# Two transformer blocks on one core: all layers in two passes over half of the tokens, with the expert rows of the first half beside the second pass

## What is computed

```python
def reference(x, ...):
    x = first_block(x, mem, ...)      # in-projection, 8 forgetting heads, 8 chunked heads, out-projection,
                                      # cross attention to a memory of 256 rows, feed-forward 1024-4096-1024
    return second_block(x, c_2, ...)  # modulation from c (6 x 1024), in-projection, sliding-window attention,
                                      # gated linear attention, out-projection, experts, last norm

def peer_ffn(h, wq, subkeys, u, v):   # the experts: 16,384 of them, 8 heads, 16 chosen by each head and token
    ...
    ub = jnp.take(u, eb, axis=0)                                   # 128 rows of 4 KB for each token
    hid = gelu(einsum('tkd,td->tk', ub, xb)) * gb
    vb = jnp.take(v, eb, axis=0)                                   # and 128 more
    return einsum('tk,tkd->td', hid, vb)
```

## Time and profile before

| what | value |
|---|---|
| median of 3 runs | 2741.86 us (2736.21 to 2760.91) |
| span of the profiled execution | 2733.2 us, clock of TensorE granted 0.935 |
| its own time beside the span | the span leaves out what lies around the program; the median of the runs is 8.7 us above it |
| PE, DVE, ACT, POOL busy | 2263.1, 1475.1, 645.8, 1188.2 us |
| moved by DMA | 665 MB, of them 537 MB by POOL's gathers |
| first gather issued, last gather issued | 1201.3 us, 2715.2 us from the start |

### The profile page before, as it was taken

How to read it: one execution, slowest core, us unless ns; L and a number is a source line. 1 busy time by engine, 2 the same in 40 slices (tenths; PEclk the granted TensorE clock), 3 DMA queues, 4 the chain that set the end, 5 groups by cost and what they waited for, 6 DMA issues and landing times.

```text
span 2733.2 us, 27506 instructions
## 1 busy us (share of the span) xinstructions
PE 2263.1 (83%) x9564; PEld 1445.1 (53%) x9564; DVE 1475.1 (54%) x3398; ACT 645.8 (24%) x1548; POOL 1188.2 (43%) x1128
## 2 busy tenths in 40 slices
PE   7999999999999999896977776767777777676775
PEld 6876888889979877665532222322223222232222
DVE  2435232375573425779866664557654567644434
ACT  3225332421120435422121111111111211111111
POOL 5200222110000221325566666666676666766664
PEclk9999999999999999898989998999988999988899
DMA  4211131144452222048889999999999999999998
GB/s 140 78 47 63 63 123 70 70 175 173 186 201 91 78 78 78 32 175 311 310 333 354 359 363 363 367 367 355 363 374 354 358 379 364 373 364 367 372 362 308
DMA packets 170936, 665.46 MB, mean 243 GB/s; under 512 B 19632, under 2 KB 20160, under 8 KB 160320
## 3 DMA queue, kind: packets, MB, share of 16 engines
q0 software_dynamic: 147456, 536.94, 52.1%
q1 hardware_dynamic: 23360, 127.00, 12.7%
HBM read 661.76 MB, written 2.10 MB: 243 GB/s over the span
## 4 chain that ended last, share of the span: by engine, by line
PE 42%; POOL 20%; DVE 15%; issue 10%; another core or an unknown queue 9%; ACT 2%; DMA 1%; SPq 0%; POOLq 0%; DVEq 0%; ACTq 0%
POOL area L544 11%; PE bank L1034 9%; PE bank L1035 9%; PE bank L1036 9%; POOL weights L535 8%; DVE weights L1925 6%; PE bank L1489 4%; PE bank L1076 2%; PE bank L1132 2%; PE bank L1187 1%; PE bank L1206 1%; PE bank L1093 1%; PE bank L1115 1%; PE bank L1099 1%
## 5 line engine op out<-in xcount | busy, mean ns | idle before, releaser
L1431 PE MATMUL bank<-area,gain_row 128*128 128x512 f32 x1888 | 967.3, 656 | 368.5 <-issue 204.2
L1431 PEld LDWEIGHTS bank<-area,gain_row 128*128 128x128 f32 x1888 | 366.6, 207 | 962.3 <-issue 824.1
L1925 DVE CUSTOM_DVE_ANT_0 weights<-weights,bank 128x1024 f32<-128x1024 f32 x504 | 596.9, 1218 | 346.7 <-DMA weights<-in_peer_u,scratch 241.0
L544 POOL DMA_INDIRECT area<-in_peer_v,scratch x512 | 491.5, 960 | 269.4 <-issue 142.3
L535 POOL DMA_INDIRECT weights<-in_peer_u,scratch x504 | 482.5, 957 | 261.4 <-issue 146.7
L918 ACT ACTIVATE gain_row<-ident,scratch 128x128 f32<-128x128 f32 x472 | 178.5, 398 | 1082.8 <-remote 588.7
L463 POOL CAST weights_split<-weights 128x2048 fp32r<-128x2048 f32 x25 | 47.7, 1906 | 851.1 <-DMA weights<-in_w_in 508.1
L1034 PE MATMUL bank<-h_T_high,weights_split 128*128 128x512 f32 (+1 forms) x544 | 211.6, 389 | 0.4 <-POOL weights_split L464 0.4
L1035 PE MATMUL bank<-h_T_low,weights_split 128*128 128x512 f32 (+1 forms) x544 | 209.7, 386 | 0.0
L1036 PE MATMUL bank<-h_T_high,weights_split 128*128 128x512 f32 (+1 forms) x544 | 209.7, 385 | 0.0
L1545 DVE CAST weights_split<-weights 128x2048 fp32r<-128x2048 f32 x41 | 50.4, 1228 | 209.0 <-DMA weights<-in_w_ff 122.8
(11 more groups left out here) (310 smaller groups left out, 3010.3 us busy)
## 6 DMA issues: line engine op xcount, KB each, us to landing
weights<-in_w_ff SPq DMA_DIRECT2D x32, 1024.0 KB, 4.8
scratch<-in_w_ada SPq DMA_DIRECT2D x48, 512.0 KB, 6.5
weights<-in_w_in SPq DMA_DIRECT2D x22, 1024.0 KB, 4.8
area<-in_w_pq SPq DMA_DIRECT2D x4, 2048.0 KB, 9.4
area<-in_peer_v,scratch POOLq DMA_INDIRECT x512
weights<-in_peer_u,scratch POOLq DMA_INDIRECT x504
weights<-in_w_mk SPq DMA_DIRECT2D x4, 1024.0 KB, 4.8
weights<-in_w_out SPq DMA_DIRECT2D x4, 1024.0 KB, 4.8
```

The costliest lines, as they stand in the source:

```text
L544: pool.indirect_dma_start(vring[k], None, A["peer_v"], index).then_inc(v_landed[k], 16)
L1431: ins = pe.matmul(bank[half][:], wdiag[:, (done + i) % 4, :], vring[r % RING][:, half * COLS:(half + 1) * COLS], start=(first and i == 0), ...
L1925: dve.tensor_tensor_reduce(out=up_slot(b, r), in0=up_slot(b, r), in1=token[b][:], scale=1.0, scalar=0.0, op0=ALU.mult, op1=ALU.add, accum_ ...
```

## The change

Two passes (p = 0, 1) of T = 256 tokens run through all layers, one after the other.

- Each pass loads all weights again, in halves of 512 KB (128 x 1024), into a ring of W_SLOTS = 4 halves. A chunk (two halves, 256 columns) serves two token blocks: 48 products of 256 columns. All products of the layers are now made by `three`, those with the memory, of the last out-projection and of the queries too. Pass 0 has 86 chunks (8 for the memory's keys and values, which are then kept in DRAM and read back in pass 1), pass 1 has 78.
- In pass 0 POOL splits the even halves and DVE the odd ones. In pass 1, while POOL issues gathers, ACT makes the high parts (`feed`, act.copy) and DVE the low ones.
- Projections are no longer woven with attention units. The far keys and values of linear attention, and its running sum and that of the forget gates, are carried to pass 1.
- The rows of blocks 0 and 1 start at the end of pass 0. In pass 1 the code of each engine is two generators, `work(1)` and `rows()`; `along` lets `work` say after each piece how many rows should have been done (`mark`, from a table of stage lengths, ROWS_WITHIN = 232 rows in the whole pass), and runs the rows up to there. The other 280 u rows come behind pass 1.
- Rings: RU = 6 slots for u, RV = 5 for v, LAG = 56. `hidden` reads the token from SBUF (token_rows).
- Modulation is done in pass 0 alone, in its feed-forward stage, with a ring of two rows. SP issues the w_ada rows of a step ahead of that step's weights.

```diff
-RING = 8
-LAG = 88
-W_SLOTS = 3
+RU, RV = 6, 5
+LAG = 56
+W_SLOTS = 4
+ROWS_WITHIN = 232
...
+        def along(work, rows):
+            n = 0
+            for want in work:
+                while n < want:
+                    next(rows)
+                    n += 1
+            for _ in rows:
+                pass
...
@@ SP, for every chunk @@
+                if p == 0 and name in ("f1", "f2"):
+                    for r in range(rows, min(48, 2 * (c - ORD[0, "f1", 0] - 1))):
+                        if r >= 2:
+                            sp.wait_ge(ada_used, r - 1)
+                        sp.dma_start(ada[:, r % 2, :], A["w_ada"][r]).then_inc(ada_landed[r % 2], 16)
+                        rows = r + 1
...
+                for h, src in enumerate(halves(c)):
+                    w = 2 * c + h
+                    if w >= W_SLOTS:
+                        sp.wait_ge(w_used if w % 2 == 0 else tile_done, (w - W_SLOTS) // 2 + 1)
...
+                    sp.dma_start(to, src).then_inc(w_landed[w % W_SLOTS], 16)
...
@@ DVE @@
+            def feed(c):
+                while fed[0] < 2 * min(c + 1, len(ORDER)):
+                    w = fed[0]
+                    fed[0] += 1
+                    raw, high, low = parts(w)
+                    if w < 2 * FIRST[1]:
+                        if w % 2 == 0:
+                            continue
+                        dve.wait_ge(w_landed[w % W_SLOTS], 16 * (w // W_SLOTS + 1))
+                        link(dve.tensor_copy(high, raw))
+                    else:
+                        dve.wait_ge(w_high, w - 2 * FIRST[1] + 1)
+                    dve.tensor_tensor(low, raw, high.bitcast(F32), ALU.subtract).then_inc(w_split, 1)
...
@@ DVE, feed-forward stage @@
+                for t, (kind, f) in enumerate(FF_ORDER):
+                    feed(ORD[p, kind, f] + 1)
+                    if kind == "f1":
+                        hidden_split(p, f)
+                    if p == 0:
+                        if t == 1:
+                            dve.wait_ge(c_ready, 1)
+                        if 1 <= t < 25:
+                            modulate(2 * t - 2)
+                            modulate(2 * t - 1)
...
-                dve.tensor_tensor_reduce(out=up_slot(b, r), in0=up_slot(b, r), in1=token[b][:], scale=1.0, scalar=0.0,
+                dve.tensor_tensor_reduce(out=uring[k], in0=uring[k], in1=token[:, b % 2, :], scale=1.0, scalar=0.0,
                                          op0=ALU.mult, op1=ALU.add, accum_out=hid[:, r:r + 1]).then_inc(u_free[k], 1)
...
-            for n in range(NB * SLOTS + LAG):
+            for n in range(ROWS + LAG):
                 if n >= LAG:
-                    down_row((n - LAG) // SLOTS, (n - LAG) % SLOTS)
-                if n < NB * SLOTS:
-                    up_row(n // SLOTS, n % SLOTS)
+                    down_row(n - LAG)
+                if n < ROWS:
+                    up_row(n)
...
+            for _ in work(0):
+                pass
+            along(work(1), rows())
```

2679 lines of the change are left out of this document (1289 added, 1390 removed).

## The result

| | before | after |
|---|---|---|
| median, 4 runs each | 2745.44 us (2736.21 to 2760.91) | 3080.94 us (3068.43 to 3083.82) |
| ratio | | 1.121, 95% interval 1.117 to 1.126 |
| span of the profiled execution, granted clock | 2733.2 us, 0.935 | 3079.2 us, 0.882 |
| first gather issued | 1201.3 us | 1038.6 us |

The account below looks back on a forecast made before the run. The prediction took PE to bound the layers and DMA the rows, one after the other. Pass 0 936, pass 1 1,030, remaining gathers 895 and the end 17 gave a 2,878 us span, 2,887 us predicted, range 2,700 to 3,010.

Parts of the forecast that it names:

- The loop in pass 0: Feed-forward stage of pass 0: w_ada issue, landing, split and modulate chained, 13.0 or 11.6 us a step; stage 341 us.
- no loop in pass 0: Rival: landings overlap the splits better, pass 0 takes 800 us, total 2,751, no change that can be told; chance 0.12.
- The lock between POOL and DVE: Pass 0's feed-forward stage: POOL's split of the even half delays DVE's odd one, 1.4 us a step.
- the three sums: Pass 1: work summed per engine, PE 750 us, DVE 777, DMA 815.
- 66 chunks at 8.2 us, bound by DMA, and 46 us of late picks: Pass 1: other chunks bound by DMA, 541 us, plus 26 pick steps delaying the next split by 1.8 us each.
- The forgetting and chunked heads of pass 1: Attention stretch in pass 1: 26 rows and other DVE work enter chains of 1.8 us a unit, 100 us.
- the upper end: Pass 1 at 1,150 us: every stage 12% longer, a lower clock for a stalling PE included.
- The other stages of pass 0: Pass 0 without its feed-forward stage: start, chunks, small products, attention, linear attention and turns, 595 us.
- The rest: Behind pass 1: 605 gathers at 1.48 us, 895 us, then 17 us to the end.
- The rival with 1.65 us a gather: POOL bounds the rest, as hidden hits gathers nearly each time; total 2,990 us, chance 0.14.
- The rows fill pass 1: Rival: waits and picks fit into slack, DMA at 364 GB/s, pass 1 870 us, total 2,666; chance 0.17.
- Chained much harder: Rival: pass 1 takes 1,150 us and more, total 3,007; chance 0.12.

Follow-up runs that it names:

- e1: Changed kernel with the block of w_ada rows issued behind the step's two weight halves: 2855.4 us, 1.101 of the kernel before.
- e9: Changed kernel without w_ada loads and the 48 modulate calls: 2846.2 us, 1.042 of the kernel before; feed-forward stage of pass 0 185 us.
- e3: Changed kernel with ACT making all high parts and DVE all low parts in pass 0, w_ada rows still ahead: 2984.0 us, 1.149 of the kernel before.
- e5: Changed kernel with w_ada rows behind the halves and ACT making all high parts in pass 0: 2836.6 us, 1.092 of the kernel before.
- e4: Changed kernel leaving out the second 512 columns of most v rows in pass 1: 2975.4 us, 1.148 of the kernel before.
- e10: Changed kernel with w_ada rows behind the halves and v row products in float32r, one record each: 2797.4 us, 1.077 of the kernel before.
- e6: Changed kernel with some 26 u rows moved out of pass 1's forgetting and chunked heads: 3071.7 us, 1.183 of the kernel before.
- the fillers: Changed kernel with three PE products whose result nobody reads added to every attention unit: 3106.2 us, 1.137 of the kernel before.
- e7: Changed kernel with hidden reading its token from PSUM for block 3 alone: 3066.0 us, 1.122 of the kernel before.
- e15: e13 with the 48 modulate calls spread over 31 steps of pass 0's feed-forward stage: 2759.2 us, 1.011 of the kernel before.
- e13: Changed kernel with w_ada rows behind, ACT's high parts, float32r row products, two unread PE products a unit in pass 1's forgetting and chunked heads, LAG = 40: 2775.9 us, 1.018.
- e16: e13 with v running 32 rows behind u instead of 40: 2768.4 us, 1.014 of the kernel before.

## Why the prediction was right and wrong

- **The loop in pass 0: right in mechanism, too small (+72 us).** The mis-sized term is the landing, 9.86 us from issue to DVE's start against 6.1. I had counted three transfers of 512 KB from the earlier trace rows; it is four, two w_ada rows and two halves, and SP itself takes 2.4 us (1.47 and 0.91) to issue them; how much each of the two adds is not shown. In the step above the landing is +3.8 us, split and lock +0.9, and the `modulate` calls -1.05, since one row can go out after the first of the two: +3.5 together, and +3.1 in the mean of the 23 steps. e1 shows the chain (-163 us by moving one block of code), e9 what a stage without it takes. The rival "no loop in pass 0" falls with it. The lock between POOL and DVE was 1.4 us a step in my sum, 32 us; the move of the splits was worth 45 us with the w_ada rows ahead (e3) and 26 with them behind (e5), and without w_ada PE never waited for a split (e9).
- **Pass 1: PE's price of a row was halved.** I read the earlier trace rows as one product where it was half of one, so PE's sum in pass 1 was 903 us and not 750 (176 rows at 1.72), the largest of the three sums. By the count of 1,888 records for 472 rows this could have been seen in the trace of before. The "128 plain products" of the last out-projection are 64 products in 128 records; its 55 us stand. The term "66 chunks at 8.2 us, bound by DMA, and 46 us of late picks" came out at 586 us against 587, and that is luck, for the mechanism is another: PE was busy with hardly a gap and no late pick held it up. e4 and e10 show it: in the feed-forward stage a chunk takes 7.7 us as soon as PE lets it, where I had put DMA at 8.2.
- **The forgetting and chunked heads of pass 1: 157 against 100 us**, which is 57 of pass 1's +81; the in-projection was 9 over, the other 15 I did not follow up. I took 1.8 us a unit from a stretch that has all four block lengths and the full clock, and used it for pass 0 (82 us together with the turn behind it, right) and pass 1 (only the two long blocks). The lower clock I had put into the upper end alone. e6 takes the rows out as a cause, and by the estimate from the fillers about 40 us are the clock; what the rest is stays open. The 26 rows that I had charged this stretch for are free there.
- **The other stages of pass 0, +28.** The in-projection took 85 us for 12 chunks (71) and the stage of the queries 62 for 8 (47): 29 us over their chunks, where I had 14 for small products, and 9 of them are the stall behind `forgets`. The other 13 us are spread, and I did not follow them up.
- **The rest: right.** 1.49 us a gather against 1.48; of the +20 us 10 are the 7 gathers more that were left. The rival with 1.65 us a gather falls. The hits of `hidden` on the gathers are there (1.09 to 1.12 us in the mean instead of 0.96) and cost nothing, as e7 shows. Here the row of before carried further than the page: the Trainium skill (SBUF — State Buffer, Who interferes with whom) infers that a VectorE instruction with two SBUF inputs leaves descriptor generation, and so the gathers, alone. The traces disagree: 1.03 us a gather with the token in SBUF, 0.95 with it in PSUM (e7).
- **The rivals.** "The rows fill pass 1" failed because PE, not the mean of three sums, was full. "Chained much harder" had the right place (1,111 us, two thirds of the way to its 1,150 and more), but I gave it 0.12 and let it stand apart from a longer loop: every term of my sum that missed was too short, and the range held only one of them missing at a time. A slip without weight: 415 rows at 1.30 us are 540 us and not 531, so a quarter of `pick` is 12.9 us and not 13.7.

**Why the idea does not pay here.** Best of all was e15, 1.011 (1.008 to 1.015) of the kernel before. No version beat it. Pass 0 has no gathers beside it (822 us at best), and the rows of blocks 2 and 3 cannot start before pass 1 ends, since their scores come from its last stage: some 600 gathers, 870 us and more, stand behind all layers, where all 1,024 stood before. In between 412 of the 1,024 gathers find cover (some more in e13 to e16), and pass 1 is 1,034 us long at best for that.

## What to carry to other kernels

- Before a time from a group's row is used as the price of an operation, divide its count of records by the number of operations in the code. A float32 product was two records here, and the price of a row doubled with it.
- A load that waits for its consumer belongs behind every load that others wait for, on the same queue: here six lines moved were worth 163 us. A change to the chunk size or the number of slots has to be read again for this order.
- A mean over a stage can be one or two gaps. Look at the single steps before a mean is used as a rate, and take the price of an attention unit from units of its own length.

## What the hardware showed beside

- The granted clock did not follow PE's busy share. In the heads of pass 0 PE was busy 35.62 of 37 us and granted 0.51, in the chunked heads of before 56.53 of 58 us at 1.00; the work is of a similar kind (here forgetting heads, with longer sums for the scores).

```profile
163.00:200.00 37.00, 35.62 (x141) 25.63 (x141) 14.50 (x64) 11.93 (x48) 1.80 (x1) 0.51 0.07 21
```

  At 0.54 PE's records also fill the time, so a busy PE can mean a slow one: here 144 of 158 us. Why the one stretch kept the clock and the other not stays open; before, it followed on heads woven with projections.
- A gather that writes float32r, with a v row rounded on its way, went as fast as one that writes float32, within 1%: the rest took 874 us in e10 and in e1, with DMA at 382 and 386 GB/s.
- A DVE cast of 128x1024 took 0.68 us at the quickest and 2.84 beside POOL's low part, and its end came 0.55 us after POOL's.
- In the rest of e10 PE was granted 0.50 for 725 us and nothing was lost against e1, where it was granted 1.00: DMA was 1.06 and 1.00 busy.
